# New addresses for the operands of two matmul stages: the output projection's at one place modulo 512 bytes, the feed-forward's eleven weight slots 64 bytes further apart

## The chip, the cores and the metric

The kernel is one program on one core of a Trainium2 chip. The metric is the device time in microseconds (us) of one execution. TensorE multiplies, VectorE and ScalarE prepare its operands and empty its results, GpSimd adds, and DMAs issued from SyncE's queue move data between device memory and SBUF.

## The reference

The input `x` is (1, 2048, 1024) in float32, and there is one layer:

```
h = rms_norm(x, norm_mix)
x = x + mixer(h @ w_in) @ w_out                 # gated linear attention, a recurrence, dilated attention
h = rms_norm(x, norm_ffn)
up = causal_dwconv(h @ ffn_w_up)                # 1024 -> 2 * 2816, three taps
u_val, u_gate = split(up, 2)
x = x + (gelu(u_gate) * u_val) @ ffn_w_down     # 2816 -> 1024
return rms_norm(x, norm_final)
```

The change touches only the product with `w_out` and the two products of the feed-forward.

## The kernel before

Every large product is made from float32 values that are split in two parts of type float32r, hi and lo, with x = hi + lo. One product of 128 contraction rows, 128 output channels and 512 tokens is three matmuls into one PSUM bank: w_hi·x_hi, w_hi·x_lo and w_lo·x_hi (helpers `product`, lines 66 to 68, and `three_passes`, lines 74 to 76). Each of the three has a load of 128 columns of weights (512 bytes in each partition, the stationary operand) and a matmul that streams 512 columns of activations (2048 bytes in each partition, the moving operand). The load for the next matmul goes on while the matmul before it streams.

The program has four parts that follow one another: the input projection with the linear attention and the recurrence (`mixer_front`, tiles `ip_`, `gl_`, `lr_`), the dilated attention (`at_`), `output_projection` (tiles `op_`) and `conv_ffn` (tiles `ff_`). A barrier of all engines stands between parts.

All places in SBUF are written out by hand as byte offsets in a partition. Those of `output_projection` and `conv_ffn` count from `FFN_ORIGIN = 9344`, which is 18 · 512 + 128. This is where the operands of TensorE stand before, in bytes modulo 512:

| tile | what TensorE does with it | offset | address mod 512 |
|---|---|---|---|
| `op_w_hi`, `op_w_lo` | weights, output projection | 0, 32768 | 128 |
| `op_w_first` | weights of the first 128 output channels, first block alone | 143392 | 160 |
| `op_mix_even_*`, `op_mix_odd_*` | moving, output projection | 159776, 92192, ... | 160 |
| `ff_b_hi`, `ff_b_lo` | moving, up product | 0, 57344 | 128 |
| `ff_ring`, slots 0 to 10, hi and lo | weights of the up product; weights and moving of the down product | 114688 + 4096 j | 128 |

Inside a tile, weights are cut at multiples of 512 bytes and moving operands at multiples of 2048, so an operand's place modulo 512 is its tile's.

`output_projection` runs over four blocks of 512 tokens, eight products of 24 matmuls each (768 matmuls). In the first block, product 0 takes its weights from `w_first`; all others take them from `w_hi` and `w_lo`.

`conv_ffn` runs over two halves of 1024 tokens. In each half the up product goes through the list `ORDER` of 154 uses of weights, each 12 matmuls against one of seven `b` tiles (seven products stand for eight, by Strassen's and Winograd's scheme), and then the down product goes through 77 steps of 12 matmuls, with one ring slot for the weights and the slot before it for the activations. Use m takes slot (m + 5·half) mod 11; step n takes slots 3 + 2(n mod 4) for the activations and 4 + 2(n mod 4) for the weights, shifted in the same way. ScalarE writes the hi part of a slot (lines 2650 and 2696), VectorE the lo part (lines 2828 and 2880), both from raw data that a DMA has brought. The order of work on each engine is written out, and semaphores tie them together.

Of the kernel before, what the change touches and what calls it, by code (L numbers as in the profile page):

```python
# [1830 lines left out]
FFN_ORIGIN = 9344  # L1831
OP_SQUARES, OP_TOTAL, OP_MIX_EVEN, OP_W_RAW, OP_MIX_IN = 84000, 88096, 159776, 192544, 208928
B00, T1, T2, B10, T3, T4, B11 = range(7)


def output_projection(nc, mix_t, x_t, w_slabs, norm_gain, rstd, x2_t, h_t, origin, w_loaded, mix_loaded, out_stored,
# [3 lines left out]
    with ExitStack() as ctx:  # L1840
# [9 lines left out]

        sb("map", [P, 217120 // 4])

# [5 lines left out]
        w_lo = placed("w_lo", [P, KT, D], 32768, F32R)  # L1858
        x_first = placed("x_first", [P, KT, NB], 67616)
        squares = placed("squares", [P, 2, NB], OP_SQUARES)  # L1860
        total = placed("total", [P, 2, NB], OP_TOTAL)
        mix_odd = [placed(f"mix_odd_{name}", [P, KT, NB], 92192 + 16384 * i, F32R) for i, name in enumerate(("hi", "lo"))]
        ones = placed("ones", [P, P], 124960)
        eps = placed("eps", [P, 1], 125472)
        gain = placed("gain", [P, KT], 125504)
        x_second = placed("x_second", [P, KT, NB], 127008)
        x_third = placed("x_third", [P, KT, NB], 143392)
        mix_hi, mix_lo = (mix_even[0], mix_odd[0]), (mix_even[1], mix_odd[1])
# [291 lines left out]
def conv_ffn(nc, x2_t, h_t, slabs, w_down, conv, gains, rstd, a_t, s_t, t_t, out_t, origin):  # L2160
# [6 lines left out]
    with ExitStack() as ctx:  # L2167
# [10 lines left out]
        RING = 11  # L2178
        SLOT = 2 * KH * P * 4
        TILE = KH * NB * 4  # L2180
# [20 lines left out]
        b_raw = placed("b_raw", [P, 7, KH, NB], at_b_lo)  # L2201
        ring = placed("ring", [P, RING, 2, KH * P], at_ring, F32R)
        raw = placed("raw", [P, 2, 4, KH * P], at_raw)
# [6 lines left out]

        raw_ring = placed("raw_ring", [P, RING, 2, KH * P], at_ring)
        x_of = [placed("x_first", [P, KT, NB], at_t + 3 * 2048 - KT * 2048), placed("x_second", [P, KT, NB], at_e)]
# [88 lines left out]
        def slot(half, m):  # L2301

            return (m + 5 * half) % RING
# [5 lines left out]
        def raw_at(half, n, i):  # L2309

            r = raw_number(half, n)
            return raw_ring[:, slot(half, r), i, :] if r < 3 else spare[:, r - 3, i, :]

# [306 lines left out]
        def _(act):  # L2620
# [12 lines left out]
            def high_w(half, m):  # L2633
                name, g = ORDER[m]
                G = PAIRS * half + g
                if name[0] == "S":
                    act.wait_ge(s_ready, 4 * G + int(name[1]))
                elif G == 0 and name == "A00":
                    act.wait_ge(first_in, 16)
                else:  # L2640
                    act.wait_ge(slab_in[g % 2], 16 * (PAIRS // 2 * half + g // 2 + 1))
                if m >= RING:
                    act.wait_ge(product_done, USES * half + m - RING + 1)
                elif half:
# [5 lines left out]
                act.activation(ring[:, slot(half, m), 0, :], source(half, m), ACT.Copy).then_inc(w_hi_ready, 1)  # L2650

# [36 lines left out]
            def high_step(half, n):  # L2688
# [6 lines left out]
                for i, to in enumerate((act_slot(half, n), weight_slot(half, n))):  # L2695
                    act.activation(ring[:, to, 0, :], raw_at(half, n, i), ACT.Copy).then_inc(d_hi_ready, 1)  # L2696

# [104 lines left out]
        def _(dve):  # L2802
# [21 lines left out]
            def low_w(half, m):  # L2824
                M = USES * half + m
                dve.wait_ge(w_hi_ready, M + 1)
                at = slot(half, m)
                dve.tensor_tensor(ring[:, at, 1, :], source(half, m), ring[:, at, 0, :].bitcast(F32),  # L2828
                                  ALU.subtract).then_inc(w_lo_ready, 1)
# [46 lines left out]
            def low_step(half, n):  # L2876
                N = STEPS * half + n
                for i, to in enumerate((act_slot(half, n), weight_slot(half, n))):
                    dve.wait_ge(d_hi_ready, 2 * N + i + 1)
                    dve.tensor_tensor(ring[:, to, 1, :], raw_at(half, n, i), ring[:, to, 0, :].bitcast(F32),  # L2880
                                      ALU.subtract).then_inc(d_lo_ready, 1)
# [84 lines left out]
        def _(pe):  # L2966
            pe.wait_ge(consts_ready, 2)

            def multiply(half, m):
# [23 lines left out]
                for k in range(KH):  # L2993
                    if g == 0:
                        pe.wait_ge(b_lo_ready, 28 * half + 4 * HI_AT[o] + k + 1)
                    cols = slice(k * P, (k + 1) * P)
                    ins = three_passes(pe, out, ring[:, at, 0, cols], ring[:, at, 1, cols], b_hi[:, o, k, :], b_lo[:, o, k, :],
                                       first and k == 0, k == KH - 1, not first)
                ins.then_inc(product_done, 1)

            def down(half, n):
# [6 lines left out]
                for o in range(OC):  # L3008
# [9 lines left out]
                    three_passes(pe, banks[OC * DOWN[q][2] + o][:, :], ring[:, weights, 0, cols], ring[:, weights, 1, cols],  # L3018
                                 ring[:, acts, 0, :], ring[:, acts, 1, :], fresh and i == 0, i == KP - 1, not fresh).then_inc(down_done, 1)

# [34 lines left out]
def program(nc, t, out_t):  # L3055
# [20 lines left out]
    def placed(name, shape, offset, dt=F32):  # L3076
        return nc.alloc_sbuf_tensor_at("op_" + name, shape, dt, offset=FFN_ORIGIN + offset)

    op_places = [placed("w_raw", [P, 2, KT, 2 * P], OP_W_RAW), placed("mix_in", [P, 4, NB], OP_MIX_IN),
                 placed("w_first", [P, 2, KT, P], 143392, F32R), placed("mix_fifth", [P, NB], 151584),  # L3080
                 [placed(f"mix_even_{name}", [P, KT, NB], OP_MIX_EVEN + 16384 * i, F32R) for i, name in enumerate(("hi", "lo"))]]
# [70 lines left out]
```

## Time and profile before

| what | value |
|---|---|
| time, median of 3 runs | 2535.85 us (2533.06 to 2538.69) |
| the profiled execution's own time | 2547.3 us |
| its span, first to last instruction | 2545.5 us |
| TensorE matmuls (PE) busy | 2438.4 us, 96% of the span |
| VectorE (DVE), ScalarE (ACT), GpSimd (POOL) busy | 67%, 44%, 39% |
| mean granted TensorE clock | 0.971 of full |
| output projection | about 1012 to 1207 us |
| feed-forward | about 1219 us to the end |

Times are in microseconds unless ns is written. PE is the matmul, PEld the load of weights, which overlaps it. A matmul's recorded duration includes its way through the array and overlaps the next one's; the rate of a stream of matmuls is read from the distance of their starts. PEclk is the granted clock of TensorE: 1.00 is 2.4 GHz, 0.50 is 1.2 GHz.

### The profile page before, as it was taken

The numbers are of one execution on the slowest core, as the hardware profiler recorded it, in microseconds if no ns is written. First come the engines' busy times: TensorE is split into PE (matmuls) and PEld (weight loads), VectorE is DVE, ScalarE is ACT, GpSimd is POOL, SyncE is SP. The second block draws the span as 40 slices with busy tenths as digits, with TensorE's granted clock in tenths as the row PEclk, the third lists the DMA queues.
The fourth block names the chain that finished last, engine by engine and source line by source line (L and its number), as shares of the span: only waits on it lengthen the run. The fifth ranks groups of instructions, "written<-read, shape, count | busy, mean of one in ns | idle before, by whom it ended". The sixth has DMA issues, their size and how long they took to land.

```text
span 2545.5 us, 33421 instructions
## 1 busy us (share of the span) xinstructions
PE 2438.4 (96%) x11968; PEld 1951.6 (77%) x11968; DVE 1711.6 (67%) x2324; ACT 1131.1 (44%) x2009; POOL 981.9 (39%) x784
## 2 busy tenths in 40 slices
PE   7999999999899998998699999999999999999997
PEld 5777877777677876776588888878777788787885
DVE  7554546776255676353678878767988888887655
ACT  6434254333045655321544444454664444444444
POOL 4111003432036774122455555413535656551211
PEclk9999989999899998999799999999999999999999
DMA  4333314443298523634422322378642322227764
GB/s 165 100 98 105 101 53 152 153 150 104 74 322 285 164 70 127 226 112 174 192 96 108 120 104 108 120 265 281 186 154 100 116 104 108 110 97 246 233 196 141
DMA packets 189445, 376.61 MB, mean 148 GB/s; under 512 B 17104, under 2 KB 61152, under 8 KB 180192
## 3 DMA queue, kind: packets, MB, share of 16 engines
q1 hardware_dynamic: 189280, 374.47, 43.4%
q8 instruction: 96, 1.57, 0.2%
q14 instruction: 69, 0.57, 0.1%
HBM read 250.43 MB, written 123.98 MB: 147 GB/s over the span
## 4 chain that ended last, share of the span: by engine, by line
PE 42%; DVE 6%; issue 1%; ACT 1%; POOL 1%; DMA 1%; SPq 0%; ACTq 0%; DVEq 0%; POOLq 0%
PE ff_bank L74 14%; PE ff_bank L76 14%; PE ff_bank L75 14%; DVE ff_y_gate L2867 2%; DVE ff_ring L2880 1%; DVE ff_ring L2828 1%; DVE ff_b_lo L2822 1%; ACT ff_y_gate L2681 0%; DMA ff_b_raw<-h_t 0%; ACT ff_e L2660 0%; DVE ff_u L2851 0%; DVE ff_u L2849 0%; DVE ff_b_raw L2813 0%; POOL ffn_rstd L2578 0%; DVE ff_y_val L2867 0%
## 5 line engine op out<-in xcount | busy, mean ns | idle before, releaser
L74 PE MATMUL ff_bank<-ff_b_hi,ff_ring 128*128 128x512 f32 x1232 | 486.3, 395 | 33.1 <-DVE ff_b_lo L2822 13.0
L76 PE MATMUL ff_bank<-ff_b_hi,ff_ring 128*128 128x512 f32 x1232 | 482.0, 391 | 0.0
L75 PE MATMUL ff_bank<-ff_b_lo,ff_ring 128*128 128x512 f32 x1232 | 481.7, 391 | 0.0
L66 PE MATMUL ip_bank<-ip_x_hi,ip_w_hi 128*128 128x512 f32 x736 | 308.9, 420 | 18.5 <-DVE ip_x_lo L708 16.2
L74 PEld LDWEIGHTS ff_bank<-ff_b_hi,ff_ring 128*128 128x128 f32 x1232 | 232.6, 189 | 97.3 <-issue 46.3
L67 PE MATMUL ip_bank<-ip_x_lo,ip_w_hi 128*128 128x512 f32 x736 | 298.7, 406 | 0.0
L68 PE MATMUL ip_bank<-ip_x_hi,ip_w_lo 128*128 128x512 f32 x736 | 297.2, 404 | 0.0
L76 PEld LDWEIGHTS ff_bank<-ff_b_hi,ff_ring 128*128 128x128 f32 x1232 | 232.6, 189 | 49.3
L75 PEld LDWEIGHTS ff_bank<-ff_b_lo,ff_ring 128*128 128x128 f32 x1232 | 232.9, 189 | 47.4 <-issue 0.2
L74 PE MATMUL ff_bank<-ff_ring 128*128 128x512 f32 x616 | 242.3, 393 | 5.4 <-DVE ff_ring L2880 5.4
L75 PE MATMUL ff_bank<-ff_ring 128*128 128x512 f32 x616 | 240.5, 390 | 0.0
L76 PE MATMUL ff_bank<-ff_ring 128*128 128x512 f32 x616 | 240.3, 390 | 0.0
L2828 DVE TENSOR_TENSOR ff_ring<-ff_raw,ff_ring 128x512 fp32r<-128x512 f32 x220 | 209.2, 957 | 41.6 <-ACT ff_ring L2650 41.6
L2880 DVE TENSOR_TENSOR ff_ring<-ff_raw_ring,ff_ring 128x512 fp32r<-128x512 f32 x196 | 151.4, 817 | 59.2 <-ACT ff_ring L2696 59.0
L66 PEld LDWEIGHTS ip_bank<-ip_x_hi,ip_w_hi 128*128 128x128 f32 x736 | 145.5, 198 | 56.9 <-issue 15.4
L723 DVE TENSOR_TENSOR ip_staged<-ip_bank,ip_rstd 128x512 f32<-128x512 f32 x80 | 54.7, 689 | 178.2 <-PE ip_bank L68 177.9
L67 PEld LDWEIGHTS ip_bank<-ip_x_lo,ip_w_hi 128*128 128x128 f32 x736 | 145.6, 198 | 32.2 <-issue 2.8
L68 PEld LDWEIGHTS ip_bank<-ip_x_hi,ip_w_lo 128*128 128x128 f32 x736 | 145.3, 197 | 32.0
L1505 ACT ACTIVATE at_probs<-at_s,at_neg 128x256 f32<-128x256 f32 (+1 forms) x288 | 107.8, 436 | 136.9 <-DVE at_neg L1593 123.0
L2696 ACT ACTIVATE ff_ring<-ff_raw_ring 128x512 fp32r<-128x512 f32 x196 | 112.9, 624 | 116.3 <-PE ff_bank L76 105.6
L2867 DVE SCALAR_TENSOR_TENSOR ff_y_gate<-ff_u,ff_conv_all,ff_y_gate 128x1024 f32<-128x1024 f32 x88 | 154.5, 1755 | 14.8 <-ACT ff_y_gate L2681 12.4
L2660 ACT ACTIVATE ff_e<-ff_bank 128x512 f32<-128x512 f32 x132 | 78.2, 592 | 172.0 <-PE ff_bank L76 161.0
(293 smaller groups left out, 4822.5 us busy)
## 6 DMA issues: line engine op xcount, KB each, us to landing
ff_raw<-in_slabs SPq DMA_DIRECT2D x43, 1024.0 KB, 4.8
proj_t<-ip_staged SPq DMA_DIRECT2D x92, 256.0 KB, 2.7
a_t<-ff_y_val SPq DMA_DIRECT2D x44, 512.0 KB, 2.6
t_t<-ff_t_sum SPq DMA_DIRECT2D x88, 256.0 KB, 2.0
ff_raw_ring<-t_t SPq DMA_DIRECT2D x56, 256.0 KB, 4.0
ff_raw_ring<-s_t SPq DMA_DIRECT2D x52, 256.0 KB, 3.3
rp_tables<-in_rope SPq DMA_DIRECT2D x24, 512.0 KB, 4.3
ip_w_raw<-in_w_in SPq DMA_DIRECT2D x23, 512.0 KB, 4.2
```

The costliest lines, as they stand in the source:

```text
L66: pe.matmul(out, w_hi[k], x_hi[k], start=(k == 0), stop=False)
L67: pe.matmul(out, w_hi[k], x_lo[k], start=False, stop=False)
L68: last = pe.matmul(out, w_lo[k], x_hi[k], start=False, stop=(k == n - 1))
L74: pe.matmul(out, w_hi, x_hi, start=first, stop=False, skip_group_check=resumed)
L75: pe.matmul(out, w_hi, x_lo, start=False, stop=False, skip_group_check=resumed)
L76: return pe.matmul(out, w_lo, x_hi, start=False, stop=last, skip_group_check=resumed)
L1505: ins = act.activation(probs[:, g, at], scores_at(j, g)[:, hh, n * c:n * (c + 1)], ACT.Exp, bias=neg[:, j % 2, c, 2 * g + hh:2 * g + hh + 1])
L2660: act.activation(e[:, i, :], banks[X[g % 2]][:, :], ACT.Copy).then_inc(e_ready[i], 1)
L2696: act.activation(ring[:, to, 0, :], raw_at(half, n, i), ACT.Copy).then_inc(d_hi_ready, 1)
L2828: dve.tensor_tensor(ring[:, at, 1, :], source(half, m), ring[:, at, 0, :].bitcast(F32), ALU.subtract).then_inc(w_lo_ready, 1)
L2867: dve.scalar_tensor_tensor(out=at, in0=u[:, a, t:t + HALF], scalar=conv_all[:, g, a, t:t + 1], in1=at, op0=ALU.mult, op1=ALU.add).then_inc ...
L2880: dve.tensor_tensor(ring[:, to, 1, :], raw_at(half, n, i), ring[:, to, 0, :].bitcast(F32), ALU.subtract).then_inc(d_lo_ready, 1)
```

## The change

It moves tiles. No instruction is added or taken away, no wait is changed, and every engine's order of work stays as it is.

In the output projection every tile behind the two weight tiles moves up by 480 bytes, so that it stands at 0 modulo 512 from the origin, as `w_hi` and `w_lo` do; `w_raw` and `mix_in` also change their order. `op_w_first` and the `mix` tiles then stand at 128 modulo 512, where `w_hi` and `w_lo` are.

In the feed-forward the ring becomes eleven tiles, 4160 bytes apart instead of 4096. Slot j then stands at 128 + 64 j modulo 512, while the `b` tiles stay at 128. All that lies behind the ring moves up by 704 bytes.

```diff
-OP_SQUARES, OP_TOTAL, OP_MIX_EVEN, OP_W_RAW, OP_MIX_IN = 84000, 88096, 159776, 192544, 208928
+OP_SQUARES, OP_TOTAL, OP_MIX_EVEN, OP_W_RAW, OP_MIX_IN = 84480, 88576, 160256, 201216, 193024
...
-        x_first = placed("x_first", [P, KT, NB], 67616)
+        x_first = placed("x_first", [P, KT, NB], 68096)
...
-        mix_odd = [placed(f"mix_odd_{name}", [P, KT, NB], 92192 + 16384 * i, F32R) for i, name in enumerate(("hi", "lo"))]
+        mix_odd = [placed(f"mix_odd_{name}", [P, KT, NB], 92672 + 16384 * i, F32R) for i, name in enumerate(("hi", "lo"))]
...
-        SLOT = 2 * KH * P * 4
+        SLOT = 2 * KH * P * 4 + 64
...
-        ring = placed("ring", [P, RING, 2, KH * P], at_ring, F32R)
+        ring = [placed(f"ring{j}", [P, 2, KH * P], at_ring + j * SLOT, F32R) for j in range(RING)]
...
-        raw_ring = placed("raw_ring", [P, RING, 2, KH * P], at_ring)
+        raw_ring = [placed(f"raw_ring{j}", [P, 2, KH * P], at_ring + j * SLOT) for j in range(RING)]
...
-                    ins = three_passes(pe, out, ring[:, at, 0, cols], ring[:, at, 1, cols], b_hi[:, o, k, :], b_lo[:, o, k, :],
+                    ins = three_passes(pe, out, ring[at][:, 0, cols], ring[at][:, 1, cols], b_hi[:, o, k, :], b_lo[:, o, k, :],
...
-                 placed("w_first", [P, 2, KT, P], 143392, F32R), placed("mix_fifth", [P, NB], 151584),
+                 placed("w_first", [P, 2, KT, P], 143872, F32R), placed("mix_fifth", [P, NB], 152064),
```

## Rows read from the trace of the kernel before

**Rows 1.** The page, part 1: busy time, share of the span, instructions.

```profile
PE 2438.4 (96%) x11968; PEld 1951.6 (77%) x11968; DVE 1711.6 (67%) x2324; ACT 1131.1 (44%) x2009; POOL 981.9 (39%) x784
```

**Rows 2.** The page, part 4: the chain that ended last, by line.

```profile
PE ff_bank L74 14%; PE ff_bank L76 14%; PE ff_bank L75 14%; DVE ff_y_gate L2867 2%; DVE ff_ring L2880 1%; DVE ff_ring L2828 1%; DVE ff_b_lo L2822 1%; ACT ff_y_gate L2681 0%; DMA ff_b_raw<-h_t 0%; ACT ff_e L2660 0%; DVE ff_u L2851 0%; DVE ff_u L2849 0%; DVE ff_b_raw L2813 0%; POOL ffn_rstd L2578 0%; DVE ff_y_val L2867 0%
```

**Rows 3.** Stretches: length, busy us (instructions) of PE, PEld, DVE, ACT, POOL, PEclk, DMA.

```profile
1100.00:1200.00 100.00, 99.17 (x422) 78.75 (x422) 37.92 (x50) 18.06 (x29) 25.78 (x18) 1.00 0.43 158
1400.00:1500.00 100.00, 100.00 (x440) 81.63 (x439) 80.53 (x83) 48.95 (x72) 59.33 (x43) 1.00 0.32 119
```

**Rows 4.** Timeline of PE, start of the output projection: start, us, engine, line.

```profile
1014.78 0.63 PE L74 MATMUL op_bank<-op_mix_even_hi,op_w_first 128*128 128x512 f32 x1
1015.20 0.63 PE L75 MATMUL op_bank<-op_mix_even_lo,op_w_first 128*128 128x512 f32 x1
...
1016.66 0.39 PE L76 MATMUL op_bank<-op_mix_even_hi,op_w_first 128*128 128x512 f32 x1
...
1017.34 0.40 PE L76 MATMUL op_bank<-op_mix_even_hi,op_w_first 128*128 128x512 f32 x1
1017.58 0.39 PE L74 MATMUL op_bank<-op_mix_even_hi,op_w_hi 128*128 128x512 f32 x1
...
1020.85 0.39 PE L76 MATMUL op_bank<-op_mix_even_hi,op_w_lo 128*128 128x512 f32 x1
```

**Rows 5.** Timeline of PE, end of the output projection; 25 starts apart.

```profile
1195.02 0.40 PE L66 MATMUL op_bank<-op_mix_odd_hi,op_w_hi 128*128 128x512 f32 x1
...
1200.85 0.39 PE L67 MATMUL op_bank<-op_mix_odd_lo,op_w_hi 128*128 128x512 f32 x1
```

**Rows 6.** Timeline of PE, up product (12 starts apart), down product (22 starts apart).

```profile
1424.19 0.39 PE L76 MATMUL ff_bank<-ff_b_hi,ff_ring 128*128 128x512 f32 x1
...
1426.91 0.39 PE L76 MATMUL ff_bank<-ff_b_hi,ff_ring 128*128 128x512 f32 x1
...
2450.01 0.39 PE L74 MATMUL ff_bank<-ff_ring 128*128 128x512 f32 x1
...
2454.99 0.39 PE L75 MATMUL ff_bank<-ff_ring 128*128 128x512 f32 x1
```

**Rows 7.** By tile: number, duration ns min/median/max, first and last start.

```profile
L66 PE MATMUL op_bank<-op_mix_odd_hi,op_w_hi x128: 393/396/794, 1063.3 to 1200.6; 128*128 128x512 f32 x128
L66 PE MATMUL op_bank<-op_mix_even_hi,op_w_hi x112: 393/396/792, 1025.2 to 1153.9; 128*128 128x512 f32 x112
L74 PE MATMUL op_bank<-op_mix_even_hi,op_w_hi x8: 393/394/397, 1017.6 to 1024.5; 128*128 128x512 f32 x8
L75 PE MATMUL ff_bank<-ff_b_lo,ff_ring x1232: 387/389/632, 1219.9 to 2313.6; 128*128 128x512 f32 x176
L75 PE MATMUL ff_bank<-ff_ring x616: 387/389/628, 1661.2 to 2525.9; 128*128 128x512 f32 x154
```

**Rows 8.** What PE waited for, output projection, then feed-forward: us in total, times, longest.

```profile
PE op_bank L66 <- DVE op_x_first L2106: 2.6, 1, 2.6
PE op_bank L66 <- DVE op_mix_odd_lo L2052: 0.8, 1, 0.8
...
PE ff_bank L74 <- ACT ff_e L2660: 7.6, 13, 2.6
```

**Rows 9.** Timeline of PE behind a short wait in the up product.

```profile
1402.46 0.47 PE L74 MATMUL ff_bank<-ff_b_hi,ff_ring 128*128 128x512 f32 x1
1402.77 0.39 PE L75 MATMUL ff_bank<-ff_b_lo,ff_ring 128*128 128x512 f32 x1
...
1404.85 0.39 PE L75 MATMUL ff_bank<-ff_b_lo,ff_ring 128*128 128x512 f32 x1
```

**Rows 10.** By tile `ff_ring`: its writers, duration ns min/median/max.

```profile
L2650 ACT ACTIVATE ff_ring<-ff_raw x220: 610/621/632, 1215.2 to 2291.9; 128x512 fp32r<-128x512 f32 x110
L2828 DVE TENSOR_TENSOR ff_ring<-ff_raw,ff_ring x220: 676/694/1792, 1215.9 to 2294.7; 128x512 fp32r<-128x512 f32 x110
```

More of the change, by code:

```diff
@@ L1849, in sem @@
             return used[-1]
-        sb("map", [P, 217120 // 4])
+        sb("map", [P, 217600 // 4])
         def placed(name, shape, offset, dt=F32):
@@ L1858, in output_projection @@
         w_lo = placed("w_lo", [P, KT, D], 32768, F32R)
-        x_first = placed("x_first", [P, KT, NB], 67616)
+        x_first = placed("x_first", [P, KT, NB], 68096)
         squares = placed("squares", [P, 2, NB], OP_SQUARES)
         total = placed("total", [P, 2, NB], OP_TOTAL)
-        mix_odd = [placed(f"mix_odd_{name}", [P, KT, NB], 92192 + 16384 * i, F32R) for i, name in enumerate(("hi", "lo"))]
[L1863 to L1867, printed above, removed]
+        mix_odd = [placed(f"mix_odd_{name}", [P, KT, NB], 92672 + 16384 * i, F32R) for i, name in enumerate(("hi", "lo"))]
+        ones = placed("ones", [P, P], 125440)
+        eps = placed("eps", [P, 1], 125952)
+        gain = placed("gain", [P, KT], 125984)
+        x_second = placed("x_second", [P, KT, NB], 127488)
+        x_third = placed("x_third", [P, KT, NB], 143872)
         mix_hi, mix_lo = (mix_even[0], mix_odd[0]), (mix_even[1], mix_odd[1])
@@ L2311, in raw_at @@
             r = raw_number(half, n)
-            return raw_ring[:, slot(half, r), i, :] if r < 3 else spare[:, r - 3, i, :]
+            return raw_ring[slot(half, r)][:, i, :] if r < 3 else spare[:, r - 3, i, :]
         def raw_before(half, n):
@@ L2649, in high_w @@
                         act.wait_ge(down_done, OC * (STEPS - 4 + ((j - 3) // 2 - STEPS) % 4 + 1))
-                act.activation(ring[:, slot(half, m), 0, :], source(half, m), ACT.Copy).then_inc(w_hi_ready, 1)
+                act.activation(ring[slot(half, m)][:, 0, :], source(half, m), ACT.Copy).then_inc(w_hi_ready, 1)
             def keep(half, g, i):
@@ L2695, in high_step @@
                 for i, to in enumerate((act_slot(half, n), weight_slot(half, n))):
-                    act.activation(ring[:, to, 0, :], raw_at(half, n, i), ACT.Copy).then_inc(d_hi_ready, 1)
+                    act.activation(ring[to][:, 0, :], raw_at(half, n, i), ACT.Copy).then_inc(d_hi_ready, 1)
             def keep_first_product(half):
@@ L2827, in low_w @@
                 at = slot(half, m)
-                dve.tensor_tensor(ring[:, at, 1, :], source(half, m), ring[:, at, 0, :].bitcast(F32),
+                dve.tensor_tensor(ring[at][:, 1, :], source(half, m), ring[at][:, 0, :].bitcast(F32),
                                   ALU.subtract).then_inc(w_lo_ready, 1)
@@ L2879, in low_step @@
                     dve.wait_ge(d_hi_ready, 2 * N + i + 1)
-                    dve.tensor_tensor(ring[:, to, 1, :], raw_at(half, n, i), ring[:, to, 0, :].bitcast(F32),
+                    dve.tensor_tensor(ring[to][:, 1, :], raw_at(half, n, i), ring[to][:, 0, :].bitcast(F32),
                                       ALU.subtract).then_inc(d_lo_ready, 1)
@@ L3017, in down @@
                     cols = slice(o * P, (o + 1) * P)
-                    three_passes(pe, banks[OC * DOWN[q][2] + o][:, :], ring[:, weights, 0, cols], ring[:, weights, 1, cols],
-                                 ring[:, acts, 0, :], ring[:, acts, 1, :], fresh and i == 0, i == KP - 1, not fresh).then_inc(down_done, 1)
+                    three_passes(pe, banks[OC * DOWN[q][2] + o][:, :], ring[weights][:, 0, cols], ring[weights][:, 1, cols],
+                                 ring[acts][:, 0, :], ring[acts][:, 1, :], fresh and i == 0, i == KP - 1, not fresh).then_inc(down_done, 1)
             def sum_squares(half, b):
```

## Prediction

> **What bounds the kernel now.** I read the page's first part to see which engine is full: TensorE's matmuls are, at 2438.4 us or 96% of the span [rows 1]. Then the chain that ended last: its largest entries by far are the three passes of the feed-forward's products, 42% together, and the next is 2% [rows 2]. Then stretches, to see whether TensorE ever stands still in the two stages that the change touches: it is busy for 99.2 of 100 us in the output projection and for all of them in the up product, at a granted clock of 1.00, which is 2.4 GHz [rows 3]. So a wait of another engine is nearly worthless here, and what counts is how far apart two matmul starts are. The timelines give that, and it is not the same everywhere:
>
> - output projection, weights `w_first`: from 1016.66 to 1017.34 there are three steps, 0.68 / 3 = 226.7 ns each [rows 4];
> - the same block directly behind it, weights `w_hi`/`w_lo`: from 1017.58 to 1020.85 there are 14 steps, 3.27 / 14 = 233.6 ns; at the stage's end 5.83 / 25 = 233.2 ns [rows 4, 5];
> - up product 2.72 / 12 = 226.7 ns, down product 4.98 / 22 = 226.4 ns [rows 6].
>
> The medians of the durations say the same, 394 to 396 ns against 389 [rows 7]. What separates the two groups is an address. In the slow one the moving operand stands at 160 modulo 512 and the weights at 128; in the fast ones both stand at the same place, be it 160 (`w_first`) or 128 (feed-forward). The step changes at once: the last matmul with `w_first`, which streams while the first part of `w_hi` is loaded, already takes 0.24 us to the next start [rows 4]. So the pair that matters is the stream of one matmul and the load of weights that goes on under it. At half clock nothing of it is left: 0.42 us from start to start, the time of 512 columns at 1.2 GHz, for the same operands [rows 4].
>
> **The change, part by part.** *Output projection.* The matmuls with `w_hi` or `w_lo` are 3 · (128 + 112 + 8) = 744, by the counts of one pass [rows 7]. After the change their operands are at equal places, as those of `w_first` are now, so I take 226.7 ns for each instead of 233.3 (the mean of the two stretches): 6.6 ns less. About ten of them run at half clock and gain nothing: 734 · 6.6 ns = 4.8 us. Not all of it arrives. TensorE waits 2.6 us near 1036 for a result that VectorE empties, held up by activations that DMAs bring [rows 8]; it would come to that wait earlier and stand longer. The some 48 matmuls between 1025.2, where product 2 begins [rows 7], and the wait give 48 · 6.6 ns = 0.3 us back. The wait of 0.8 us for the low part of the last block's activations [rows 8] hangs on VectorE's work behind the product before; that product is shorter by 24 · 6.6 ns = 0.16 us, and this is given back too. Everything behind TensorE's end of the stage (a sum, the root, the barrier, the first loads of the feed-forward) starts from it and moves with it. Sum: -4.8 + 0.3 + 0.2 = -4.3 us. Bounds: 0 if the place is not the cause, -4.9 if nothing is given back.
>
> The page "SBUF — State Buffer" of the Trainium skill says in "Who interferes with whom" that TensorE has separate read ports for the moving operand and for loading weights and never waits on anyone. By that rule this part would be worth 0 us and so would the next; the 6.6 ns between two runs of matmuls in one stage speak against it. The same page, in "Door 1: The DMA port swizzle", gives SBUF lines of 16 bytes, by which 32 bytes apart would be a whole number of lines and as good as 0; the trace disagrees there too.
>
> *Feed-forward.* This part changes where weights stand against the moving operand, and the trace has no row for what it makes: distances of 64 to 448 bytes. First the counts. Up product: 2 · 154 uses of 12 matmuls, 3696 (3 · 1232, [rows 7]); slots 0 and 8 of the eleven stay equal to `b` modulo 512, 672 matmuls, and 3024 become unequal. Down product: both operands lie in the ring, 3 · 616 = 1848 matmuls, weights one slot further than activations (64 bytes), in some 384: all unequal. Together 4872 that change, against 734 in the output projection. One nanosecond on each is 4.9 us, so this part decides the result if it does anything at all.
>
> What a changed matmul costs, bounded from both sides: if any unequal place is as bad as 32 bytes apart, +6.6 ns [rows 4, 5]. If the distance brings the stream closer to undisturbed, the floor is 512 columns at 2.4 GHz, half of the half-clock step of 0.427 (1.2 GHz for 512 columns), 213.3 ns: -13.4 ns. Which value? The load of weights passes 512 bytes while the stream passes 2048, so whatever memory line two reads can meet in, the stream overtakes the load through all the 512 bytes of differences in any case; a head start by whole lines changes only when they meet, while a head start by part of a line changes how their fetches fall against each other. 32 bytes apart is seen to matter, so a line would be longer than 32 bytes; 64 is the next power of two, and 64 j then is a whole number of lines. So I take +0 ns, the row of equal places, as the likeliest. This is an argument and no measurement, and the rivals below are nearly as likely.
>
> The other work on the ring: ScalarE writes a slot in 610 to 632 ns, and VectorE's fastest is 676 ns with a median of 694 [rows 10]; the range of ScalarE's is so narrow, with TensorE reading other slots at the same place modulo 512, that there is no conflict for a new spacing to cure. What lies behind the ring (`raw`, `s`, `e`, `u`, `y`) moves 704 bytes and is no operand of a large product. No instruction, semaphore or DMA is added, so no wait is either: 0 us.
>
> **The sum.** -4.3 + 0 = -4.3 us against the profiled execution's 2547.3 us (a span of 2545.5 and 1.8 around it): 2543.0 us. That execution lies 11.45 us above the median of the runs, so the forecast for the median is 2535.85 - 4.3 = 2531.5 us, 0.17% faster. About 0.2% (5.1 us) is what a measurement of this kernel can tell from no change, so this is at the edge.
>
> **The rivals.**
>
> 1. *Every unequal place costs what 32 bytes apart cost.* For it: the only unequal distance in the trace costs 6.6 ns, and the fast step looks like a state that equal places fall into, since behind a short wait the up product needs nine matmuls at 2.08 / 9 = 231 ns before it is at 226.7 again [rows 9]. Against it: the argument of whole lines. Price: 4872 · 6.6 ns = +32.2 us, all on TensorE's path. A little is taken back where TensorE now waits: 7.6 us for `ff_e` in 13 waits [rows 8], whose ends mostly move along, so perhaps 1 us. 2535.85 - 4.3 + 31 = 2562.6 us, slower by 1.1%. It decides the sign from 0.9 ns per changed matmul (4.3 us / 4872).
> 2. *Only some distances cost.* If lines of 128 bytes count, odd slots pay in the up product (5 of 11, 1680 matmuls) and all pay in the down product: 3528 · 6.6 ns = +23.3 us, 2554.8 us. If only the down product pays (1848), +12.2 us, 2543.7. If each of the 308 uses has to settle anew, as behind a wait, 308 · 9 · (231 - 226.7) ns = +11.9 us, 2543.5 us. I take 2545 for the group.
> 3. *Unequal whole lines are better than equal ones.* For it: an equal-place matmul still takes 13.4 ns more than its 512 columns, and the settling matmuls behind a wait show that the step is no constant. Against it: nothing in the trace is faster than 226.4. Price at half of the room: 4872 · 6.7 ns = -32.6 us, 2498.9 us; slower feeding by VectorE (80.5 us busy of 100 [rows 3]) would take part of it, so 2505.
> 4. *The places do nothing in either stage* (the step in the output projection has another cause): 2535.85 us. The change of step in the middle of one block, between two sets of weights alone, speaks against it [rows 4].
>
> For rival 3 a page of the skill has a price as well: "TensorE: Matmul & The Clock Gate", in "Wait — 56ns, not 53.3ns?", measures 215.7 ns for back-to-back 512-column matmuls at full clock. By that figure the estimate of the most that could be had is 4872 · 11 ns = 53.6 us. No row here shows it.
>
> **How the numbers follow.** Chances: forecast 0.43, rival 1 0.24, rival 2 0.13, rival 3 0.17, rival 4 0.03. The predicted time is the forecast's, 2531.5 us; its own range is 2528 to 2535 (bounds of the first part and the noise of a median). To hold 8 in 10 the range goes up to rival 1 with its full price, 2565, and down to where rival 3 would still be with the first few nanoseconds of its gain, 2508. Faster by over 0.2% means below 2530.8: rival 3 and four tenths of the forecast, 0.34. Slower means above 2540.9: rival 1 and nearly all of rival 2, 0.36. Within 0.2%: the rest, 0.30.
>
> **What would show it.** In the profile after, the output projection's matmuls should have a median of 389 ns instead of 396, with starts 226.7 ns apart, and TensorE's wait near 1036 should be some 0.3 us longer. If they stay at 396, the place is not the cause. In the feed-forward the step should stay at 226.7 in both products; read slot by slot, it says at once which rival holds: 233 in all but two slots of eleven is rival 1, a pattern of odd slots or the down product alone is rival 2, anything below 226 is rival 3. The durations of ScalarE's and VectorE's writes to the ring should not move. The forecast goes wrong above all if fetches of the two streams do not repeat every 64 bytes.

## The result, and the profile after

| | median of 8 runs | lowest to highest |
|---|---|---|
| before | 2540.61 us | 2530.58 to 2544.95 |
| after | 2557.23 us | 2550.82 to 2562.41 |

The ratio is 1.0071, with a 95% interval of [1.0052, 1.009]: 0.71% slower, about 18 us by the ratio; the two medians are 16.6 us apart. The forecast was 4.3 us faster.

The page of the changed kernel, part 1 and the chain by line, against [rows 1, 2]:

```profile
PE 2445.6 (96%) x11968; PEld 1946.9 (76%) x11968; DVE 1707.2 (67%) x2324; ACT 1130.6 (44%) x2009; POOL 975.9 (38%) x784
...
PE ff_bank L74 15%; PE ff_bank L76 15%; PE ff_bank L75 15%; DVE ff_y_gate L2867 1%; DVE ff_ring L2880 1%; DVE ff_b_lo L2822 1%; DMA ff_b_raw<-h_t 0%; ACT ff_ring L2696 0%; ACT ff_e L2660 0%; DVE ff_u L2851 0%; DVE ff_b_raw L2813 0%; POOL ffn_rstd L2578 0%; DVE ff_ring L2828 0%; DVE ff_u L2849 0%; DVE ff_x_first L2901 0%
```

All that grew is TensorE: 7.2 us more busy with the same number of matmuls (20.0 us more in the feed-forward, 1280.2 to 1300.2, and less in the stages before it), and its three passes of the feed-forward now hold 45% of the chain instead of 42%. The other engines are busy as long as before, or a little shorter. By stages in the two traces (us); the output projection is counted to the end of the sum that closes it, and 13.0 us without a matmul follow it in both:

| stage | before | after | difference |
|---|---|---|---|
| up to the end of the input projection | 701.4 | 692.5 | -8.9 |
| attention | 310.7 | 312.5 | +1.8 |
| output projection | 194.3 | 191.2 | -3.1 |
| up product, first half | 441.6 | 451.6 | +10.0 |
| down product, first half | 218.1 | 222.5 | +4.4 |
| up product, second half | 434.9 | 434.4 | -0.5 |
| down product, second half | 212.5 | 217.3 | +4.8 |

The first two stages are untouched by the change, and their 7 us are the difference of two executions (the granted clock was 0.971 in one and 0.974 in the other). What belongs to the change is -3.1 us in the output projection and +18.7 us in the feed-forward.

*Output projection.* The end of the stage as the timeline of TensorE shows it, 27 starts apart, and two groups by tile (number, ns min/median/max), against [rows 5, 7]:

```profile
1179.68 0.39 PE L66 MATMUL op_bank<-op_mix_odd_hi,op_w_hi 128*128 128x512 f32 x1
...
1185.81 0.39 PE L66 MATMUL op_bank<-op_mix_odd_hi,op_w_hi 128*128 128x512 f32 x1
```

```profile
L66 PE MATMUL op_bank<-op_mix_odd_hi,op_w_hi x128: 387/389/799, 1053.9 to 1190.6; 128*128 128x512 f32 x128
...
L75 PE MATMUL ff_bank<-ff_b_lo,ff_ring x1232: 387/393/628, 1209.8 to 2317.3; 128*128 128x512 f32 x176
...
L75 PE MATMUL ff_bank<-ff_ring,ff_ring x616: 388/394/398, 1661.1 to 2534.5; 128*128 128x512 f32 x154
```

6.13 us / 27 = 227.0 ns a step instead of 233.2 [rows 5], and a median of 389 ns instead of 396: the two groups of matmuls have changed places, for the feed-forward's medians went from 389 to 393 and 394. What TensorE waited for (total, times, longest), against [rows 8]:

```profile
PE op_bank L66 <- DVE op_x_first L2106: 2.8, 1, 2.8
...
PE op_bank L66 <- DVE op_mix_odd_lo L2052: 2.2, 1, 2.2
```

The first wait grew by 0.2 us, the second by 1.4 us. So 1.6 us went back to waits where 0.5 had been expected. Only the second is clear of chance: the first was 3.4 us long in the kernel with the ring alone (below), where the output projection is as before.

*Feed-forward, slot by slot.* Every twelfth start in the up product is the first of one use of a slot. From the first line on the slots are 4, 5, ... 10, 0; the weights lie 256, 320, 384, 448, 0, 64 and 128 bytes behind the moving operand modulo 512:

```profile
1422.96 0.39 PE L74 MATMUL ff_bank<-ff_b_hi,ff_ring 128*128 128x512 f32 x1
...
1425.69 0.40 PE L74 MATMUL ff_bank<-ff_b_hi,ff_ring 128*128 128x512 f32 x1
...
1428.49 0.39 PE L74 MATMUL ff_bank<-ff_b_hi,ff_ring 128*128 128x512 f32 x1
...
1431.28 0.39 PE L74 MATMUL ff_bank<-ff_b_hi,ff_ring 128*128 128x512 f32 x1
...
1434.03 0.39 PE L74 MATMUL ff_bank<-ff_b_hi,ff_ring 128*128 128x512 f32 x1
...
1436.76 0.40 PE L74 MATMUL ff_bank<-ff_b_hi,ff_ring 128*128 128x512 f32 x1
...
1439.56 0.39 PE L74 MATMUL ff_bank<-ff_b_hi,ff_ring 128*128 128x512 f32 x1
...
1442.36 0.39 PE L74 MATMUL ff_bank<-ff_b_hi,ff_ring 128*128 128x512 f32 x1
```

The twelve steps take 2.73 us at distances 256 and 0, 2.75 at 448, and 2.79 or 2.80 at 320, 384, 64 and 128. Averaged over all uses of the slots (the distances between the first eleven pairs of starts in each use; starts over 245 ns apart, waits and half clock, left out):

| distance, bytes | 0 | 64 | 128 | 192 | 256 | 320 | 384 | 448 |
|---|---|---|---|---|---|---|---|---|
| mean step, ns | 227.8 | 233.6 | 232.9 | 229.2 | 227.9 | 233.5 | 232.9 | 229.1 |

The second four repeat the first four within 0.1 ns: the pattern has a period of 256 bytes. The mean over all steps of the up product is 230.9 ns where it was 227.0, and over the down product 232.6 where it was 226.9. ScalarE's and VectorE's writes to the ring are as in [rows 10]:

```profile
L2650 ACT ACTIVATE ff_ring<-ff_raw x220: 609/620/633, 1205.0 to 2295.3; 128x512 fp32r<-128x512 f32 x110
...
L2828 DVE TENSOR_TENSOR ff_ring<-ff_raw,ff_ring x220: 675/693/1789, 1205.6 to 2298.2; 128x512 fp32r<-128x512 f32 x110
```

### The profile page after: what moved, and what is told of

It is laid out like the page before. It is cut to its first block, busy times and chain, and to the rows that moved or that the text cites. A ratio compares the mean times of both kernels' runs of the same rounds, so it can differ in the third digit from the quotient of the medians.

```text
span 2554.0 us, 33421 instructions
## 1 busy us (share of the span) xinstructions
PE 2445.6 (96%) x11968; PEld 1946.9 (76%) x11968; DVE 1707.2 (67%) x2324; ACT 1130.6 (44%) x2009; POOL 975.9 (38%) x784
## 4 chain that ended last, share of the span: by engine, by line
PE 45%; DVE 4%; issue 2%; ACT 1%; DMA 1%; POOL 0%; ACTq 0%; SPq 0%; DVEq 0%; POOLq 0%
PE ff_bank L74 15%; PE ff_bank L76 15%; PE ff_bank L75 15%; DVE ff_y_gate L2867 1%; DVE ff_ring L2880 1%; DVE ff_b_lo L2822 1%; DMA ff_b_raw<-h_t 0%; ACT ff_ring L2696 0%; ACT ff_e L2660 0%; DVE ff_u L2851 0%; DVE ff_b_raw L2813 0%; POOL ffn_rstd L2578 0%; DVE ff_ring L2828 0%; DVE ff_u L2849 0%; DVE ff_x_first L2901 0%
## 5 line engine op out<-in xcount | busy, mean ns | idle before, releaser
L74 PEld LDWEIGHTS ff_bank<-ff_b_hi,ff_ring 128*128 128x128 f32 x1232 | 233.1, 189 | 96.3 <-issue 40.9
L76 PEld LDWEIGHTS ff_bank<-ff_b_hi,ff_ring 128*128 128x128 f32 x1232 | 232.8, 189 | 53.8
L75 PEld LDWEIGHTS ff_bank<-ff_b_lo,ff_ring 128*128 128x128 f32 x1232 | 233.3, 189 | 52.6 <-issue 0.2
L74 PE MATMUL ff_bank<-ff_ring,ff_ring 128*128 128x512 f32 x616 | 244.6, 397 | 5.7 <-DVE ff_ring L2880 5.7
L76 PE MATMUL ff_bank<-ff_ring,ff_ring 128*128 128x512 f32 x616 | 243.1, 395 | 0.0
L75 PE MATMUL ff_bank<-ff_ring,ff_ring 128*128 128x512 f32 x616 | 243.0, 394 | 0.0
```

The lines of the kernel that those rows point to most:

```text
L74: pe.matmul(out, w_hi, x_hi, start=first, stop=False, skip_group_check=resumed)
L75: pe.matmul(out, w_hi, x_lo, start=False, stop=False, skip_group_check=resumed)
L76: return pe.matmul(out, w_lo, x_hi, start=False, stop=last, skip_group_check=resumed)
```

## The experiments

Steps are worked out everywhere as in the table above. "Settled" means the last five of the eleven steps of a use alone.

### The two parts apart

*The output projection alone*. The ring goes back to 4096 bytes a slot:

```diff
-        SLOT = 2 * KH * P * 4 + 64
+        SLOT = 2 * KH * P * 4
```

> The output projection's tiles at their new places, the ring's slots 4096 bytes apart as before. Theory A (the step from matmul to matmul depends on the distance between weights and moving operand alone, and equal places give 226.7 ns): the output projection's steps stay at 226.7 ns as in the changed kernel, both feed-forward products go back to 226.7 to 227.1 ns, and the time is 3 to 5 us below the kernel before, a ratio of 0.998 to 0.999. Theory B (the gain of the output projection is lost again in waits, so that the part is worth nothing): ratio 1.000 with its steps at 226.7 ns and waits in the output projection longer by 4 us.

*The ring alone*. The output projection's offsets are those of before, the ring that of the changed kernel:

```diff
-OP_SQUARES, OP_TOTAL, OP_MIX_EVEN, OP_W_RAW, OP_MIX_IN = 84480, 88576, 160256, 201216, 193024
+OP_SQUARES, OP_TOTAL, OP_MIX_EVEN, OP_W_RAW, OP_MIX_IN = 84000, 88096, 159776, 192544, 208928
...
```

> The output projection's tiles at their old places (steps of 233.3 ns again), the ring's slots 4160 bytes apart as in the changed kernel. By the steps of the changed kernel the up product costs 3.9 ns more in each of about 3600 matmuls at full clock, 14.0 us, and the down product 5.7 ns in each of about 1830, 10.4 us: 24.4 us in all. Theory A (steps add up): ratio to the kernel before 1.0095. Theory B (waits of the up product in which TensorE stood anyway take a part back, since some of them end with work that does not follow TensorE): 15 to 20 us, ratio 1.006 to 1.008, with the busy steps as in the changed kernel and less waiting behind them.

| kernel | median, us | before, us | ratio [95%] |
|---|---|---|---|
| output projection alone | 2535.80 (12 runs) | 2540.71 (17) | 0.9982 [0.9967, 0.9996] |
| ring alone | 2560.48 (6 runs) | 2540.71 (17) | 1.0072 [1.005, 1.0094] |

By tile, the output projection's matmuls in the first kernel and in the second:

```profile
L66 PE MATMUL op_bank<-op_mix_odd_hi,op_w_hi x128: 387/389/799, 1061.3 to 1196.3; 128*128 128x512 f32 x128
```

```profile
L66 PE MATMUL op_bank<-op_mix_odd_hi,op_w_hi x128: 393/396/794, 1058.8 to 1196.1; 128*128 128x512 f32 x128
```

The first kernel came out as theory A has it, the second as theory B does: the loss is there, and waits take part of it back. (By time alone theory A's 1.0095 lies only just outside the second kernel's interval; the stages below, 19.1 us or 1.0075, decide it.) The first part is worth 4.6 us by the ratio (0.18% of 2540.7, with an interval of 1.0 to 8.4 us), and 3.1 us in the profile: from the first matmul of the output projection to the first of the up product it takes 204.2 us instead of 207.3, as in the changed kernel. The whole loss is the ring's: 18.3 us by the ratio. The kernel with the first part alone is faster than both. The two parts add up to 13.7 us by the ratios and 16.0 by the stages, where the whole change gave 18.0 (interval 13.2 to 22.9) and 15.6; the difference is within what the runs can tell.

The ring's steps alone give more than that. Against before, the up product's 3.9 ns on some 3,600 matmuls at full clock are 14.0 us, and the down product's 5.7 ns on some 1,830 are 10.4 us, 24.4 together; the four stages grew by 9.5 + 3.6 + 1.2 + 4.8 = 19.1 us. Where the rest went is seen in the second half's up product. Two stretches, the first and second half's up product (length, busy us of PE, PEld, DVE, ACT, POOL, PEclk), for the ring alone:

```profile
1214.90:1666.00 451.10, 435.16 (x1849) 350.71 (x1850) 354.85 (x377) 215.49 (x324) 239.24 (x172) 0.98 0.30 114
...
1887.60:2323.70 436.10, 431.86 (x1851) 347.30 (x1850) 351.61 (x358) 204.79 (x299) 240.26 (x174) 1.00 0.29 108
```

and for the same stretches of the kernel before:

```profile
1219.30:1660.90 441.60, 428.77 (x1848) 349.58 (x1849) 352.72 (x377) 215.72 (x324) 242.37 (x172) 0.98 0.31 117
...
1879.00:2314.00 435.00, 426.09 (x1852) 345.46 (x1851) 358.57 (x361) 204.76 (x299) 241.40 (x174) 1.00 0.30 109
```

In the second half TensorE is busy 5.8 us longer and the stretch is only 1.1 us longer: its idle time fell from 8.9 us to 4.2, and its waits for ScalarE's `ff_e` from 11 (6.3 us) to 3 (3.9 us). The chain of a stretch in the middle says why. Before, it leads through VectorE's and ScalarE's work on the results (its shares by line, and two of its instructions):

```profile
by line: PE ff_bank L74 26.1%; PE ff_bank L76 24.9%; PE ff_bank L75 24.8%; DVE ff_y_gate L2867 7.7%; issue 5.3%; DVE ff_ring L2828 4.7%; ACT ff_y_gate L2681 3.4%; DVE ff_u L2849 1.9%; DVE ff_u L2851 1.9%; ACT ff_e L2660 1.6%; ACTq L2643 0.1
...
2021.89 1.26 ACT ff_y_gate L2681
...
2060.89 1.26 ACT ff_y_gate L2681
```

With the ring alone it is TensorE's own:

```profile
by line: PE ff_bank L74 33.8%; PE ff_bank L76 33.2%; PE ff_bank L75 33.1%; issue 0.1%
...
2041.43 0.43 PE ff_bank L74
...
2080.42 0.47 PE ff_bank L74
...
2119.43 0.47 PE ff_bank L74
```

Both return every 39.0 us, two groups of the up product. By these chains TensorE stood still before for part of each 39.0 us because the loop through VectorE, which ends in the wait for `ff_e`, took that long; the slower steps filled the time it had stood still. That is read from the chains and from the unchanged 39.0 us; no run changed the loop itself. In the first half it is the other way round. TensorE alone made the chain of 1450 to 1560 us before (33.8, 33.3 and 33.0% for its three lines), and two groups took 38.4 us. With the ring alone they take 39.6 us, and the chain has VectorE in it again:

```profile
by line: PE ff_bank L74 24.0%; PE ff_bank L76 23.4%; PE ff_bank L75 23.3%; DVE ff_y_gate L2867 12.4%; issue 10.2%; DVE ff_u L2851 1.9%; ACT ff_ring L2650 1.7%; ACT ff_e L2660 1.6%; DVE ff_u L2849 1.3%; DVE ff_ring L2828 0.2%; ACTq L2643 0.1
```

TensorE's idle time there grew from 12.8 to 15.9 us, and its waits for `ff_e` from 2 (1.4 us) to 8 (4.9 us). So the 7 us of slower steps that each half of the up product has became 9.5 and 1.2 us. The down product's 10.4 us became 8.4; its idle time fell by 1.4 us, and the rest has no account. Why the loop closes in one half and opens in the other was not tried.

### Which distances cost

*Slots 32 bytes apart*, one run. It adds the odd multiples of 32:

```diff
-        ring = [placed(f"ring{j}", [P, 2, KH * P], at_ring + j * SLOT, F32R) for j in range(RING)]
+        ring = [placed(f"ring{j}", [P, 2, KH * P], at_ring + j * (SLOT - 32), F32R) for j in range(RING)]
...
```

> Slots 4128 bytes apart: distances 0, 32, ..., 320 bytes from the b tiles in the up product, and 32 bytes between activations and weights in the down product (-320 at the end of the ring). Theory A (period of 256 bytes): 0 and 256 at 227 to 228 ns, 64 and 320 at 233.5, 128 at 233, 192 at 229, 32 and 288 alike and near the 233.3 that the output projection had at a distance of 32; distances of 96, 160 and 224 somewhere between their neighbours. Theory B (a period of 512 bytes with a second good place at 256 by chance): 32 and 288, 64 and 320 would differ. Theory C (only whole lines matter, and 32 is a broken line): all odd multiples of 32 at 233 ns or above, whatever their neighbours.

The time was 2554.98 us, beside a median of 2540.71 before. Every twelfth start of the up product; the four uses between these lines have distances 224, 256, 288 and 320:

```profile
1430.97 0.40 PE L74 MATMUL ff_bank<-ff_b_hi,ff_ring 128*128 128x512 f32 x1
...
1433.76 0.39 PE L74 MATMUL ff_bank<-ff_b_hi,ff_ring 128*128 128x512 f32 x1
...
1436.49 0.39 PE L74 MATMUL ff_bank<-ff_b_hi,ff_ring 128*128 128x512 f32 x1
...
1439.28 0.40 PE L74 MATMUL ff_bank<-ff_b_hi,ff_ring 128*128 128x512 f32 x1
...
1442.08 0.39 PE L74 MATMUL ff_bank<-ff_b_hi,ff_ring 128*128 128x512 f32 x1
```

2.79, 2.73, 2.79 and 2.80 us. Over all uses:

| distance | 0 | 32 | 64 | 96 | 128 | 160 | 192 | 224 | 256 | 288 | 320 |
|---|---|---|---|---|---|---|---|---|---|---|---|
| mean step, ns | 229.3 | 232.9 | 233.5 | 233.7 | 232.1 | 233.5 | 229.7 | 233.4 | 226.8 | 232.9 | 233.5 |

(Distance 0 has 226.9 once it has settled.) 32 and 288 agree, as do 64 and 320, 0 and 256, so the period of 256 holds, which is theory A. Its other half, that 96, 160 and 224 lie between their neighbours, failed: they take 233.4 to 233.7 ns, above both. In this theory C was right, that all odd multiples of 32 cost the same (32 and 288 too, at 233.6 and 233.7 once settled), though not for its reason, since the whole multiples of 64 are slow as well. One slot out of place, 32 bytes from 256, costs 6 ns.

*Fine distances*, one run. The slots stand at 0, 4, 8, 16, 24, 48, 80, 144, 208, 240 and 252 bytes:

```diff
+        FINE = (0, 4, 8, 16, 24, 48, 80, 144, 208, 240, 252)
...
+                extra = FINE[j] % 32 // 4
+                tile = placed(f"{name}{j}", [P, 2 * KH * P + extra], at_ring + 4096 * j + FINE[j] // 32 * 32, dt)
+                made.append(tile[:, extra:].rearrange("p (i c) -> p i c", i=2))
```

> Slots at distances of 0, 4, 8, 16, 24, 48, 80, 144, 208, 240 and 252 bytes from the b tiles. Theory A (a smooth rise from the equal place): 4 and 252 bytes near 227 to 228 ns, 8 and 16 between 228 and 232, 24 and 48 near 233, 240 and 252 back towards 227. Theory B (fetches by lines of 16 or 32 bytes or more: the place within a line does not count by itself but any broken line does): a jump to 231 to 234 ns at 4 bytes already, and the same on the other side at 252.

The time was 2558.34 us, beside 2540.71.

| distance, up product | 0 | 4 | 8 | 16 | 24 | 48 | 80 | 144 | 208 | 240 | 252 |
|---|---|---|---|---|---|---|---|---|---|---|---|
| mean step, ns | 227.4 | 232.4 | 230.6 | 233.1 | 230.3 | 233.2 | 231.8 | 233.2 | 231.8 | 228.6 | 229.4 |

The step jumps by 5 ns for four bytes (theory B) and then goes up and down with no slope, which neither theory had said; at 252 bytes it stays below theory B's 231. That value is a mixture: over their last six steps 16 of the 28 uses at 252 average 226.7 ns and 12 average 233.3. So there is no line of 32 or 64 bytes within which places are as good as equal. The down product has both operands in the ring, and there the same distance of 32 gives 226.8 ns for activations at 48 and weights at 80, and 229.4 ns for 208 and 240. So the distance is not all that counts.

*A grid of places*, one run. Each of the seven `b` tiles has a place of its own, and the slots stand 16 bytes apart; the block of `b_lo` and the ring move up by 256 and 512 bytes to make room:

```diff
+        FINE = (0, 16, 32, 48, 64, 80, 96, 112, 128, 144, 160)
+        B_FINE = (0, 16, 32, 48, 64, 96, 128)
...
```

> The seven b tiles stand at 0, 16, 32, 48, 64, 96 and 128 bytes modulo 256 from their old place and the eleven slots at 0, 16, ..., 160, so that the up product tries 77 pairs of places, some 48 matmuls each. Theory A (the step depends on the distance modulo 256 alone): all pairs of one distance agree, at 226.7 to 228 ns for distance 0, 232 to 233.5 for 32 to 128, whatever the place of the moving operand. Theory B (the moving operand's own place modulo 32 or 64 counts too, as the down product with slots at 48 and 80 suggests, which ran at 226.8 ns with a distance of 32): pairs of one distance differ by up to 6 ns with the place of b, and distance 0 is at 226.7 only where b is at a multiple of 32. Theory C (there are pairs better than equal places): some pair settles below 226 ns.

The time was 2564.82 us, beside 2539.31 for one run of the kernel before. Settled step in ns; rows are the place of `b`, columns that of the weights:

| b | 0 | 16 | 32 | 48 | 64 | 80 | 96 | 112 | 128 | 144 | 160 |
|---|---|---|---|---|---|---|---|---|---|---|---|
| 0 | 226.9 | 233.7 | 233.2 | 233.2 | 233.3 | 232.0 | 234.7 | 233.4 | 233.4 | 233.8 | 233.8 |
| 16 | 231.6 | 229.6 | 234.7 | 226.7 | 234.7 | 229.8 | 233.2 | 229.7 | 233.3 | 232.8 | 229.8 |
| 32 | 233.5 | 227.6 | 229.5 | 233.0 | 233.0 | 233.4 | 233.3 | 232.0 | 233.6 | 233.3 | 232.7 |
| 48 | 233.7 | 232.2 | 231.3 | 230.9 | 236.2 | 226.7 | 234.8 | 228.5 | 233.3 | 226.6 | 233.3 |
| 64 | 229.5 | 232.2 | 233.4 | 227.6 | 227.8 | 231.6 | 233.5 | 233.3 | 233.6 | 232.0 | 234.6 |
| 96 | 232.8 | 229.9 | 228.9 | 231.3 | 233.7 | 227.6 | 229.0 | 231.7 | 233.8 | 233.2 | 233.3 |
| 128 | 233.6 | 234.1 | 233.7 | 229.9 | 228.9 | 231.3 | 233.5 | 228.5 | 226.7 | 233.6 | 233.2 |

Most pairs take 231 to 235 ns. A few unequal ones are as fast as the best equal ones (16 with 48, 48 with 80, 48 with 144). None of the 77 is below 226.6. Theory B holds and C falls.

The table must be read with two reservations. First, a use has only twelve matmuls, and some pairs haven't settled by its last five steps. The uses of 32 with 32 and of 96 with 96 go through 236, 228, 232 and 231 ns and are at 226 or 227 from their tenth step on, so equal places at a multiple of 32 all end at 226.7, and the 229.5 and 229.0 are averages on the way there. Second, one pair can settle in more than one way. These are two uses of `b` at 64 with the weights at 80, from the sixth start to the twelfth:

```profile
1403.20 0.39 PE L76 MATMUL ff_bank<-ff_b_hi,ff_ring 128*128 128x512 f32 x1
...
1404.61 0.39 PE L76 MATMUL ff_bank<-ff_b_hi,ff_ring 128*128 128x512 f32 x1
```

```profile
1621.24 0.39 PE L76 MATMUL ff_bank<-ff_b_hi,ff_ring 128*128 128x512 f32 x1
...
1622.61 0.40 PE L76 MATMUL ff_bank<-ff_b_hi,ff_ring 128*128 128x512 f32 x1
```

Six steps take 1.41 us in the first and 1.37 in the second: 233.3 and 226.7 ns by the trace's own digits, and of this pair's four uses three are slow and one is fast. It is the same for 96 with 112, and in 10 of the 77 pairs the uses lie more than 1.5 ns apart. So the two places don't fix the step by themselves; something of what goes before a use has a part in it, and no run isolates that.

### Is it the distance, or the change of slots?

*All slots at 64*, one run. Every use has the same place, so nothing has to settle anew from slot to slot; in the down product both operands stand at the same place again:

```diff
-        ring = [placed(f"ring{j}", [P, 2, KH * P], at_ring + j * SLOT, F32R) for j in range(RING)]
+        ring = [placed(f"ring{j}", [P, 2, KH * P], at_ring + 64 + j * (SLOT - 64), F32R) for j in range(RING)]
...
```

> All slots 4096 bytes apart, the whole ring 64 bytes further: the up product has a distance of 64 bytes throughout, the down product 0. Theory A (the distance sets the step): up product 233.5 ns in all uses, down product 226.7 to 227. Theory B (what costs is the change of the distance from one use of weights to the next, after which the step has to settle, 64 bytes being whole lines): the up product settles at 226.7 to 227 ns since nothing changes any more, and the down product likewise.

The time was 2562.62 us beside 2539.31. By tile, an up and a down group:

```profile
L75 PE MATMUL ff_bank<-ff_b_lo,ff_ring x1232: 388/394/628, 1217.0 to 2329.3; 128*128 128x512 f32 x176
...
L75 PE MATMUL ff_bank<-ff_ring,ff_ring x616: 387/389/398, 1670.0 to 2541.3; 128*128 128x512 f32 x154
```

The up product is at 394 ns (a step of 233.3), the down product at 389 (226.9), in one kernel and on one ring. The distance of 64 bytes makes the cost (theory A), without any change of place from use to use.

*256 bytes apart*. The ring and all that stands behind the output projection's weights lie 256 bytes further than in the first experiment:

```diff
+        ring = [placed(f"ring{j}", [P, 2, KH * P], at_ring + 256 + j * (SLOT - 64), F32R) for j in range(RING)]
...
+OP_SQUARES, OP_TOTAL, OP_MIX_EVEN, OP_W_RAW, OP_MIX_IN = 84736, 88832, 160512, 201472, 193280
```

> In the output projection the moving operands stand 256 bytes modulo 512 from w_hi and w_lo, in the up product the ring stands 256 bytes from b; nothing is equal modulo 512, the down product excepted. Theory A (the rule has a period of 256 bytes): all three products at 226.7 to 227 ns and the time of the kernel with the output projection's places alone, a ratio of 0.998 to the kernel before. Theory B (equal places modulo 512 are needed, and the good values at 256 bytes in the spaced ring come from the short stay there): output projection and up product at 229 to 233 ns, 15 to 25 us above the kernel before in the up product alone.

The median was 2537.51 us (12 runs) against 2539.11 (17): 0.9994 [0.998, 1.0008]. The steps are 227.0 ns in both products of the feed-forward, and the output projection's group is that of the first experiment:

```profile
L66 PE MATMUL op_bank<-op_mix_odd_hi,op_w_hi x128: 387/389/799, 1047.3 to 1182.4; 128*128 128x512 f32 x128
```

So 256 bytes apart is as good as equal, in the 3,696 matmuls of the up product and in the output projection (in the down product both operands lie in the ring and are equal again). That is theory A by the steps. Its time can't be told from that of the kernel before, nor from 0.9982: the two intervals overlap.

*Equal, but at 16 modulo 32*, one run. `b` and all slots stand 16 bytes further than a multiple of 32, at distance 0:

```diff
+        FINE = (16, 16, 16, 16, 16, 16, 16, 16, 16, 16, 16)
+        B_FINE = (16, 16, 16, 16, 16, 16, 16)
...
```

> All b tiles and all slots stand 16 bytes further, so that the distance is 0 everywhere, at places that are 16 modulo 32. Theory A (only the distance counts once the step has settled): 226.7 to 227 ns in the up and the down product. Theory B (the moving operand's own place modulo 32 counts too): another step, near the 229.6 ns that this pair had in the grid, in both products, some 3 ns by 5500 matmuls or 15 us more.

The time was 2553.62 us beside 2539.11. By tile:

```profile
L75 PE MATMUL ff_bank<-ff_b_lo,ff_ring x1232: 389/396/632, 1204.9 to 2316.0; 128*128 128x512 f32 x176
...
L75 PE MATMUL ff_bank<-ff_ring,ff_ring x616: 389/394/397, 1656.8 to 2532.3; 128*128 128x512 f32 x154
```

The steps are 232.3 and 231.3 ns. Equal places are not enough (theory B): they must also stand on 32 bytes, or this pair is nearly as slow as most unequal ones. The 229.6 ns of the grid did not come back. With every use at one pair, the last six steps of a use in the up product still average 233.3 ns in 187 of the 308 uses, 231 in 61 and 230.0 in 56: here too one pair of places has several steps.

## Why the prediction was wrong

The step that failed is the price of an unequal place in the feed-forward: "64 j then is a whole number of lines. So I take +0 ns". The runs put 3.9 ns on a matmul of the up product (4.7 on each of those whose distance changed) and 5.7 ns on one of the down product, in place of 0, and the sum's second term is +18.3 us by the ring alone, in place of 0. The forecast said itself that the +0 was an argument and no measurement.

Point by point:

- *What bounds the kernel*: right. A few nanoseconds on a step are all that the change did, and they came out as 18 us.
- *The output projection, -4.3 us*: right in sign and cause. The runs give -4.6 us by the ratio and -3.1 us in the profile, and the smaller one is what the measured terms come to: the step fell by 6.3 ns, 4.6 us in all, but 1.6 us went back to waits instead of 0.5. Of these 1.4 are at the wait for the low part of the last block, which had been costed at 0.2, as though all but one product's gain would reach its end. Counted from the stage's first matmul, TensorE came to this wait 4.8 us earlier and left it 3.4 us earlier (3.2 and 1.8 us with this part alone). The count before the wait near 1036 was short as well: the second product's 24 matmuls with `w_hi` and `w_lo`, before 1025.2, gain too, which makes 72 matmuls and 0.5 us, not 48 and 0.3.
- *That places decide, through the load under a stream*: that places decide is right, by the step in two stages that changed places while instructions, waits and writers stayed the same. That the load under the stream is the partner is not shown. Before, the last matmul with `w_first`, with `w_hi` loaded under it, takes 235 ns both times it comes up; but in the changed kernel the last matmul of a use of slot 4, under which slot 5's weights are loaded 64 bytes further, still takes 225 or 226 ns, and the slow steps begin one matmul later. "Equal modulo 512" was too narrow and too wide at once: the period is 256 bytes, and equal places off 32 bytes are slow.
- *At half clock nothing of it is left*: true, but not by the rows named. Those are of `w_first`, whose operands stood at equal places. The same block has the unequal pair at half clock too, four steps in 1.71 us, 0.43 us each:

```profile
1041.12 0.63 PE L66 MATMUL op_bank<-op_mix_even_hi,op_w_hi 128*128 128x512 f32 x1
...
1042.83 0.63 PE L67 MATMUL op_bank<-op_mix_even_lo,op_w_hi 128*128 128x512 f32 x1
```

- *Whole lines are neutral*: wrong for 64 bytes. The only multiple of 32 that is as good as 0 is 256. The argument that the stream overtakes the load through all differences anyway, so that a head start only moves their meeting, falls with it: a distance that is the same in every matmul keeps its price in every matmul (233.3 ns with all slots at 64).
- *Rival 1*, every unequal place costs 6.6 ns, came nearest and named the mechanism. Its price was too high in two terms. 256 costs nothing, and 192 and 448 only 2 ns, so the steps gave 24.4 us and not 32.2; and of these 19.1 arrived in the stages, 5.3 less, where 1 us had been allowed. The waits for `ff_e` named there were the right place to look, but what they gave back depends on the half: the up product's second half took 5.9 us less than its slower steps, most of it time in which TensorE had stood still in the 39.0 us loop, and its first half took 2.4 us more.
- *Rival 2* has a part of the truth, in that distances differ, but not by its rule of odd slots: 128 costs nearly what 64 does (232.9 and 233.6 ns).
- *Rival 3*, unequal places faster than equal ones: no pair of the grid settled below 226.6 ns, the step of equal places. The page "TensorE: Matmul & The Clock Gate" of the Trainium skill gives 215.7 ns in "Wait — 56ns, not 53.3ns?"; no placement tried here came below 226.6.
- *Rival 4*: refuted, by both parts.
- *Settling* in each use, the last part of rival 2, is real but a small price: at distances of 0 and 256 the changed kernel's uses average 227.8 ns where they settle at 226.8, which is about 0.9 us of the up product's 14.0. With all slots at 64 nothing has to settle anew, and the step is 233.3 ns all the same.

The page "SBUF — State Buffer" of the Trainium skill names lines of 16 bytes in "Door 1: The DMA port swizzle". Four bytes of distance cost 5 ns here, and equal places 16 bytes on cost 5 ns, so what the two reads of TensorE meet in is not told by that line.

Left open: what in the chip makes the pattern. It has a period of 256 bytes and a special place for distance 0 on multiples of 32, and no rule was found that gives the rest of the grid. Open too is what decides between the steps that one pair of places can have: the pair before it, a wait, or accesses of other engines could, and none of these was tried.

## What to carry to other kernels

Where TensorE is full, compare the distance between starts, not busy shares, from stage to stage: 3% between two stages with the same shapes is a sign that operands stand badly. Put the moving operand and its weights at the same place modulo 256 bytes, on a multiple of 32, as every such pair here ended at 226.7 ns. Any other pair has to be tried over a long stretch and not over twelve matmuls: a distance that looks harmless cost 2 to 7 ns a matmul here, and the same pair could be fast in one use and slow in the next. Of this change the output projection's half is to be kept (0.9982 [0.9967, 0.9996]) and the ring's spacing to be dropped.

## What the runs showed of the hardware that was not expected

- The step of a float32r matmul of 512 columns, with a load of 128 columns under it, lies between 226.6 and 236.5 ns at a granted clock of 1.00 with instructions and shapes unchanged, by where its two operands stand (the highest is the down product of the fine distances, activations at 4 and weights at 8 bytes). At half clock it is 427 ns for equal places and for 32 and 64 bytes apart.
- The pattern repeats every 256 bytes (0 and 256: 227.8 and 227.9 ns; 64 and 320: 233.6 and 233.5; 128 and 384: 232.9 both; 192 and 448: 229.2 and 229.1).
- Four bytes of distance are enough (232.4 ns), and the moving operand's own place counts too: 232.3 ns for equal places at 16 modulo 32, and 226.7 for 16 with 48 in three uses of the grid.
- One pair of places can have more than one step: 64 with 80 took 233.3 ns in three uses and 226.7 in one, equal places at 16 modulo 32 took 233.3, 231 and 230.0.
- A slower TensorE can cost little: 5.8 us more busy time in the second half's up product moved its end by 1.1 us.
